# One more matmul, whose result nobody reads, ahead of 28 groups of 256-column products

## What is computed

```
def swiglu(h, wg, wu, wd):
    return (jax.nn.silu(h @ wg) * (h @ wu)) @ wd

x = x + swiglu(rms_norm(x, norm_ffn[layer]), ffn_w_gate[i], ffn_w_up[i], ffn_w_down[i])
```

## Time and profile before

| | |
|---|---|
| Median of three runs | 1374.54 us (1374.29 to 1374.68) |
| Profiled execution, first to last instruction | 1372.6 us |
| Median less that span | 1.9 us |
| PE busy, share of the span | 1354.2 us, 99% |
| DVE, ACT busy | 1180.1 us (86%), 1017.8 us (74%) |
| Granted TensorE clock, mean | 1.000 (2.4 GHz) |
| 256-column products of the feed-forward block | 134.8 us to 280.3 us, 864 |

### The profile page before, as it was taken

One profiled execution on the slowest core, in us unless ns is written; L12 is line 12 of the kernel. 1 busy time (PEld: TensorE's weight loads), 2 busy tenths in 40 slices (PEclk: granted clock), 3 DMA queues, 4 the chain that ended last, 5 costly groups with the idle time before them and its releaser, 6 DMA issues.

```text
span 1372.6 us, 19885 instructions
## 1 busy us (share of the span) xinstructions
PE 1354.2 (99%) x6885; PEld 1139.1 (83%) x6885; DVE 1180.1 (86%) x1369; ACT 1017.8 (74%) x1189; POOL 133.2 (10%) x132
## 2 busy tenths in 40 slices
PE   9999999999998999999999999999999999999998
PEld 7778999988987788888888888888888888888886
DVE  5876555568959999999999999999999999999998
ACT  5656444456757778888888888888888888888886
POOL 1020000000222240200200110020020002003000
PEclk9999999999999999999999999999999999999999
DMA  9944543643656999999999999999999999999980
GB/s 346 361 144 162 184 154 123 229 139 123 246 217 254 363 373 372 383 395 375 369 394 397 354 391 398 369 372 394 392 354 391 400 368 371 395 387 356 394 335 31
DMA packets 184623, 430.89 MB, mean 314 GB/s; under 512 B 6076, under 2 KB 14032, under 8 KB 184576
## 3 DMA queue, kind: packets, MB, share of 16 engines
q1 hardware_dynamic: 181136, 422.81, 82.8%
q0 software_dynamic: 3440, 7.44, 2.5%
HBM read 425.68 MB, written 7.36 MB: 315 GB/s over the span
## 4 chain that ended last, share of the span: by engine, by line
PE 90%; DVE 6%; DMA 1%; issue 1%; ACT 1%; POOL 0%; DVEq 0%; SPq 0%; POOLq 0%; ACTq 0%
PE psum L788 29%; PE psum L790 28%; PE psum L789 28%; DVE w_lo L428 2%; PE psum L1360 2%; DVE w_lo L410 1%; DMA slot_table<-routing,table_row 1%; DMA routing<-slot_table 0%; PE psum L820 0%; PE psum L921 0%; POOL slot_table L712 0%; DVE probs L2114 0%; PE psum L1062 0%; DMA const<-const_f 0%; PE psum L953 0%
## 5 line engine op out<-in xcount | busy, mean ns | idle before, releaser
L428 DVE TENSOR_TENSOR w_lo<-raw_ring,w_hi 128x1024 fp32r<-128x1024 f32 x674 | 811.2, 1228 | 49.0 <-ACT w_hi L423 12.1
L423 ACT ACTIVATE w_hi<-raw_ring 128x1024 fp32r<-128x1024 f32 x675 | 713.1, 1062 | 169.3 <-PE psum L790 168.4
L788 PE MATMUL psum<-w_hi,xg_hi 128*128 128x512 f32 x896 | 351.4, 392 | 4.2 <-DVE w_lo L428 4.1
L790 PE MATMUL psum<-w_hi,xg_lo 128*128 128x512 f32 x896 | 349.0, 390 | 0.0
L789 PE MATMUL psum<-w_lo,xg_hi 128*128 128x512 f32 x896 | 348.7, 389 | 0.0
L410 DVE TENSOR_TENSOR w_lo<-raw_ring,w_hi 128x1024 fp32r<-128x1024 f32 x124 | 151.3, 1227 | 78.0 <-ACT w_hi L402 77.1
L788 PEld LDWEIGHTS psum<-w_hi,xg_hi 128*128 128x128 f32 x896 | 168.2, 188 | 40.0 <-DVE w_lo L428 4.1
L402 ACT ACTIVATE w_hi<-raw_ring 128x1024 fp32r<-128x1024 f32 x124 | 130.0, 1058 | 93.9 <-PE psum L790 93.6
L790 PEld LDWEIGHTS psum<-w_hi,xg_lo 128*128 128x128 f32 x896 | 168.2, 188 | 35.4
L789 PEld LDWEIGHTS psum<-w_lo,xg_hi 128*128 128x128 f32 x896 | 168.3, 188 | 34.1
L788 PE MATMUL psum<-w_hi,moe_hT_hi 128*128 128x512 f32 x448 | 175.7, 392 | 0.7 <-DVE w_lo L428 0.7
(11 more groups left out here) (299 smaller groups left out, 1348.4 us busy)
## 6 DMA issues: line engine op xcount, KB each, us to landing
raw_ring<-in_moe_w_gate SPq DMA_DIRECT2D x56, 2048.0 KB, 10.4
raw_ring<-in_moe_w_up SPq DMA_DIRECT2D x56, 2048.0 KB, 11.0
raw_ring<-in_moe_w_down SPq DMA_DIRECT2D x56, 2048.0 KB, 10.1
raw_ring<-in_ffn_w_gate SPq DMA_DIRECT2D x5, 2048.0 KB, 12.5
raw_ring<-in_ffn_w_up SPq DMA_DIRECT2D x5, 2048.0 KB, 8.9
raw_ring<-in_ffn_w_down SPq DMA_DIRECT2D x5, 2048.0 KB, 10.3
raw_ring<-in_w_in_ab SPq DMA_DIRECT2D x4, 2048.0 KB, 19.4
raw_ring<-in_w_in_cd SPq DMA_DIRECT2D x4, 2048.0 KB, 8.0
```

What stands on the lines that cost most here:

```text
L423: act.activation(wh[:, v % SPLITS, :], moe_raw(i, q), ACT.Copy).then_inc(hi_ready, 1)
L428: dve.tensor_tensor(wl[:, v % SPLITS, :], moe_raw(i, q), wh[:, v % SPLITS, :].bitcast(F32), ALU.subtract).then_inc(lo_ready, 1)
L788: pe.matmul(out_, sh, mh_, start=start, stop=False)
L790: return pe.matmul(out_, sl, mh_, start=False, stop=stop)
```

## The change

A function `shift_phase` is added, and `ffn()` calls it ahead of every group of slabs 2 to 5, behind the group's two waits. It issues one matmul whose stationary operand is the first block of `ffn_hi` and whose moving operand is the first `cols` columns of `ffn_hi`, into the bank that the group then overwrites from the start. Nothing reads its result. The table has 32 widths; slab 5 has only four groups, so the last four entries (240, 448, 480, 512) are not used, and 28 are.

```
+SHIFTS = ((272, 288, 304, 320, 336, 352, 368, 384),
+          (288, 272, 320, 304, 352, 336, 384, 368),
+          (264, 280, 296, 312, 328, 344, 360, 376),
+          (64, 128, 192, 224, 240, 448, 480, 512))
...
+            def shift_phase(b, cols):
+
+                flat = ffn_hi[:, 0:2, :].rearrange("p k f -> p (k f)")
+                pe.matmul(bank(b, cols), ffn_hi[:, 0, 0:P], flat[:, 0:cols], start=True, stop=True)
...
                             pe.wait_ge(lo_ready, u + 1)
+                            if s >= 2:
+                                shift_phase(2 * which + b % 2, SHIFTS[s - 2][2 * bb + which])
                             for k in range(KD):
```

## The result

Over 17 runs each, the changed kernel takes 1376.95 us and the kernel before 1374.76 us (medians); the ratio is 1.0019, with a 95% interval of 1.0012 to 1.0025. So it is slower by 1.6 to 3.4 us. The prediction had 1378.1 us, with 1375.3 to 1379.3 as its range. The time lies in the range. The case that I had called the likeliest did not come true: a rival did.

What follows compares the result with a forecast made beforehand. PE alone was taken to bound the feed-forward block. New products cost 3.9 us, 0.3 us comes back from narrow ones' groups: 3.6 us added to the median 1374.54 gives 1378.1 us, range 1375.3 to 1379.3.

Steps and rivals of the forecast that it cites:

- the likeliest: Groups behind the 24 products of 264 to 384 columns keep 117.8 ns; cost 3.2 to 4.3 us; chance 47%.
- PE alone sets the pace, and what follows moves as a whole: Feed-forward block, 134.70 to 292.60 us: PE busy throughout, so added PE time delays its end and all later stages equally.
- The new products cost 3.9 us: 28 unread products on PE: 24 wide (264 to 384 columns) 3.46 us, four narrow (64 to 224) 0.45 us.
- So I expect the 24 wide ones to leave the pitch as it is: Slabs 2 to 4: products over 256 columns let the next load finish, so groups behind stay at 117.8 ns.
- tight: Faster pitch of the 256-column products, 113.3 ns, read in slab 1 behind narrow transposes.
- Most of the four narrow ones to tighten their groups: Slab 5: products of 64 to 224 columns make PE stand, giving back up to 0.4 us, 0.3 taken.
- loose: Slower pitch of the 256-column products, 117.8 ns, read in slabs 2 and 5 behind 512-column products.
- part of the wide products tighten: Rival, slabs 2 to 5: 11 to 20 of 28 groups at 113.3 ns, cost 2.7 to 1.8 us; 22%.
- It is dearer: Rival: groups slow to 120 ns, or each new product adds 0.10 us; 5.4 or 6.7 us in all; 12%.
- it vanishes later: Rival, experts' stage: waits for split weights absorb up to 3.6 us, giving 1374.5 to 1375; 5%, including anything unseen.
- The rule of two independent read ports: Skill page: loading takes no bandwidth from the running product; then no group would tighten and the sum would be 3.9 us.
- all tight: Rival: any other width breaks the 117.8 ns pattern at all 28 places; cost 0.9 us, time 1375.4; 14%.

Runs made afterwards that it cites:

- -128: Kernel before, no unread products, feed-forward inputs 64 bytes lower (FFN_PHASE -128 instead of -64): block 165.45 us, +2.64; slab 2 at 120.0 ns a product.
- -96: Kernel before, no unread products, feed-forward inputs 32 bytes lower (FFN_PHASE -96 instead of -64): block 164.43 us, +1.62; slab 2 at 118.7 ns a product.
- -32: Kernel before, no unread products, feed-forward inputs 32 bytes higher (FFN_PHASE -32 instead of -64): block 164.29 us, +1.48; slab 2 at 118.3 ns a product.

## Why the prediction was right in its number and wrong in its likeliest case

- *PE alone sets the pace, and what follows moves as a whole:* right. The block's 2.74 us are PE's, and PE's work in the later stages is what it was.
- *The new products cost 3.9 us:* 3.88 us to the next start, the wide ones 3.60 and the narrow ones 0.29. I had 3.46 and 0.45, so that the sum agrees because two misses cancel. The missing 0.16 us of the narrow ones are in the start behind them; with it each costs 0.11 us, as I took it, and all 28 cost 4.05 us. A wide one is a little dearer than its columns: 384 columns have 188.82 - 188.64 = 0.18 us for an expected 0.170.
- *"So I expect the 24 wide ones to leave the pitch as it is":* this step failed, and the largest error is here. I had 0.3 us coming back, from narrow products alone; 1.19 us came back. Thirteen of the 24 wide groups became tight. I had argued from the width: a long product lets the next load finish, as the down products do, so the group would start as it starts now. But at the first group of a slab the width is not what matters: with the group's own operands 256 and 272 columns both leave slab 2 at 22.61 us, and with another loaded address 256 columns make it 21.78. I had looked at the time that a load has, and not at where it reads. Three of the thirteen are such first groups. The other ten lie inside a slab, where the width does count (behind a tight group 272 columns led to loose and 288 to tight), and their cause stays open.
- *"Most of the four narrow ones to tighten their groups":* failed too. Two of four did (128 and 192), and the four groups of slab 5 together gave back nothing, since it went into the starts. The longest stand, 0.20 us behind the 64-column product, which is that of the earlier trace rows to the hundredth, was followed by a loose group. A stand of PE does not by itself make a stream tight. Nor was slab 1 tight only behind its transposes, as I had read it: its second group, ahead of them, has 2.73 us (137.70 to 140.43).
- *The rival "part of the wide products tighten":* this is what happened, with its size a little off. Its 1376.3 to 1377.4 us hold the measured time. It had 107 ns a group; the thirteen tight groups behind wide products give back about 92 ns each (1.20 us in all), since most start with a few slower products, and the two behind narrow ones give back no more than the loose groups of slab 5 lose. With 15 groups it would have had 3.9 - 1.6 = 2.3 us; the trace has 2.74.
- *"It is dearer" and "it vanishes later":* neither. No group in the changed kernel slowed to 120 ns, though the run with -128 shows that this pitch exists for the block too.
- *The rule of two independent read ports* in the Trainium skill, "TensorE: Matmul & The Clock Gate", section "Step-by-step: what each phase is for", by which the load takes nothing from the running product: the runs do not fit it here. With the streams unchanged, moving the block that one unread product loads by 64 bytes takes the 192 products behind it from 22.61 to 21.78 us. Moving the inputs by 32 bytes also takes the pitch from 113.3 or 117.8 to 118.3 or 118.7 ns, but that could be the stream's own affair. That load and stream meet on the way to PE is a guess of mine; no row shows it, and a load that is itself slower at some addresses is not excluded.
- *The number and the range:* the number was near in part by luck. The sum had 3.6 us and the block grew by 2.74, and a range that began at the price of "all tight" would have held the time whichever groups tightened, so it says nothing for the mechanism. Two of the prediction's ends also don't follow from its terms: the likeliest case ends at 1378.8, not at 1379.3, and 11 tight groups give 1374.54 + 2.7 = 1377.2, not 1377.4. The measured 1376.95 is inside either way.

**What stays open.** The map is known for few of its cases. Behind the down products every product tried that loads from `ffn_hi` with 256 to 288 columns led to tight, and 64 columns to loose; inside a slab the result depends on width and state together (352 columns: loose behind a tight group, tight behind a loose one), and I can't derive the 28 results from a rule. Nor do the runs show by which step of the address the effect repeats; 512 bytes is a multiple of it, 32 and 64 are not. The sizes of the buffers in the kernel put `ffn_hi` 192 bytes beyond a multiple of 512 from the blocks of `w_hi`, and 160, 128 and 224 with -96, -128 and -32. Counted modulo 128 that is 64 (113.3 and 117.8 ns), 32 (118.7), 0 (120.0) and 96 (118.3); `act_hi`, with 120 ns in the earlier trace rows (there as the loaded operand), is at 0 too, and of the unread products of 256 columns tried behind the down products those that load at 0 led to loose and those at 32 and 64 to tight. So a step of 128 bytes would fit, but no run tests it.

## What to carry to other kernels

Where PE is the bound and its matmuls are short enough that the next load takes nearly as long as the stream (here some 0.11 us of each), read the pitch over each stretch, and not the duration of a row or the busy share: 113.3 and 117.8 ns here both show as 100% busy with a duration of 0.28 us. If the same product has two pitches, look at what stands just ahead of the faster stretch, and at the addresses of the loaded and the streamed operand modulo 512 bytes; one unread product with its loaded block moved by 32 or 64 bytes, at the start of a stretch and not before every group, was worth 2.4 us in this kernel. A disturbance that repairs the state at one place can spoil it at the next, as 256 and 272 columns before every group did, so put in no more of them than there are bad entrances.

## What the runs showed of the hardware that I had not expected

- A stream of 256-column products at the 2.4 GHz level has several steady pitches: 113.3, 117.8, 118.3, 118.7 and 120.0 ns in slab 2, by the addresses of its operands and by how it began. It keeps one for 192 products without drifting.
- It is deterministic: two executions of the changed kernel agree group by group, 28 results out of 28.
- The 512-column down products wipe the state: behind them the same start gives the same result, whether the slab ahead was tight (the run with one product for each slab) or loose (the runs with 28 of one width). They themselves settle at 226.7 ns every time, within some ten products.
